# Two of four weighted sums on VectorE, and a ring that grows by a row in each tile

## The reference, cut to what matters

```
q    = (hc @ w_q).reshape(128, 8, 2, 128)                 # per tile of 128 tokens
sc   = einsum("chpd,pkd->chpk", q, subkeys)               # key scores, 2 x 128 per head
...                                                       # top 16 of each half, top 16 of their 256 sums
eidx = take_along_axis(cand_idx, top_pos)                 # 8 heads x 16 = 128 experts per token
gate = softmax(top_s)
act  = gelu(einsum("chkd,cd->chk", u_tab[eidx], hc))
out  = einsum("chk,chkd->cd", gate * act, v_tab[eidx])
```

## Time and profile before

| | |
|---|---|
| time of the kernel, median of 2 runs | 6663.14 us (6650.19 to 6676.09) |
| the profiled execution's own time | 6652.61 us |
| its span, first to last instruction | 6650.8 us |
| PE busy | 4862.6 us (73%) |
| VectorE busy | 3565.7 us (54%) |
| ScalarE busy | 849.4 us (13%) |
| GpSimd busy | 1459.3 us (22%) |
| mean rate of transfers over the span | 227 GB/s |
| gathers (queue q0) | 1342.26 MB |
| mean granted TensorE clock | 0.85 of full speed |

### The profile page before, as it was taken

One profiled execution on the slowest core, in us unless ns is written; L12 is line 12 of the kernel. 1 busy time (PEld: TensorE's weight loads), 2 busy tenths in 40 slices (PEclk: granted clock), 3 DMA queues, 4 the chain that ended last, 5 costly groups with the idle time before them and its releaser, 6 DMA issues.

```text
span 6650.8 us, 45921 instructions
## 1 busy us (share of the span) xinstructions
PE 4862.6 (73%) x14848; PEld 2726.0 (41%) x14848; DVE 3565.7 (54%) x7774; ACT 849.4 (13%) x2368; POOL 1459.3 (22%) x1310
## 2 busy tenths in 40 slices
PE   5989999966666666665579899989566666666564
PEld 3856677722222222222248567777222222222221
DVE  0755111477767677764408451114776776777544
ACT  1133000111111001110011330011111011011100
POOL 0000000033333333334300000000333333333343
PEclk8989999977777777777789899999777777777777
DMA  5100111079899988988741001110898889988886
GB/s 219 45 26 1 56 59 64 31 306 347 348 350 353 352 345 348 353 344 325 292 182 36 26 1 62 62 60 26 347 353 345 345 345 349 351 342 349 346 328 260
DMA packets 213697, 1509.71 MB, mean 227 GB/s; under 512 B 24657, under 2 KB 26961, under 8 KB 37073
## 3 DMA queue, kind: packets, MB, share of 16 engines
q0 software_dynamic: 184320, 1342.26, 52.0%
q1 hardware_dynamic: 29136, 164.52, 6.8%
HBM read 1503.54 MB, written 3.15 MB: 227 GB/s over the span
## 4 chain that ended last, share of the span: by engine, by line
PE 36%; DMA 30%; issue 12%; DVE 10%; POOL 9%; ACT 2%; DVEq 0%; SPq 0%; POOLq 0%; ACTq 0%
DMA B<-tables,R 22%; POOL B L367 9%; PE ps L600 8%; DMA R<-tables,R 6%; DVE hT L1239 4%; PE ps L440 4%; PE ps L605 4%; PE ps L657 4%; DVE B L1209 4%; PE ps L425 2%; PE ps L619 2%; DMA B<-ws 2%; PE ps L537 2%; PE ps L524 1%; PE ps L677 1%
## 5 line engine op out<-in xcount | busy, mean ns | idle before, releaser
L677 PE MATMUL ps<-B,hT 128*128 128x512 f32 x3328 | 2086.2, 790 | 1219.2 <-ACT hT L872 1219.2
L367 POOL DMA_INDIRECT B<-tables,R x1152 | 1293.7, 1123 | 4010.0 <-DVE hT L1239 2076.7
L1209 DVE SCALAR_TENSOR_TENSOR B<-B,M 128x1024 f32<-128x1024 f32 x1152 | 1389.0, 1224 | 1002.4 <-DMA B<-tables,R 971.8
L677 PEld LDWEIGHTS ps<-B,hT 128*128 128x128 f32 x3328 | 838.8, 261 | 2494.3 <-ACT hT L872 1393.1
L677 PE MATMUL ps<-R,hT 128*128 128x512 f32 x512 | 350.2, 822 | 296.7 <-ACT hT L872 296.7
L600 PE MATMUL ps<-hT,B 128*128 128x320 f32 x2048 | 561.9, 432 | 1.4 <-ACT R L831 1.4
L866 ACT ACTIVATE T<-T 128x4 f32<-128x4 f32 x320 | 66.3, 207 | 3066.7 <-DVEq L1211 3066.7
L600 PEld LDWEIGHTS ps<-hT,B 128*128 128x128 f32 x2048 | 389.0, 190 | 164.9 <-ACT R L831 3.0
L1239 DVE SCALAR_TENSOR_TENSOR hT<-B,skT,hT 128x1024 f32<-128x1024 f32 x310 | 398.1, 1284 | 40.4 <-issue 0.5
L872 ACT ACTIVATE hT<-cs,skT 128x128 f32<-128x128 f32 x960 | 317.3, 394 | 412.4 <-DVEq L1229 412.4
L1103 DVE TENSOR_TENSOR A<-ps,A 128x640 f32<-128x640 f32 x48 | 39.6, 825 | 551.2 <-PE ps L605 551.2
(11 more groups left out here) (197 smaller groups left out, 3996.3 us busy)
## 6 DMA issues: line engine op xcount, KB each, us to landing
B<-ws SPq DMA_DIRECT2D x96, 1024.0 KB, 4.9
B<-ws SPq DMA_DIRECT2D x64, 768.0 KB, 4.1
B<-tables,R POOLq DMA_INDIRECT x1152
R<-tabs SPq DMA_DIRECT2D x2, 2176.0 KB, 8.2
x<-xin SPq DMA_DIRECT2D x1, 2560.0 KB, 9.2
y<-M SPq DMA_DIRECT2D x1, 2560.0 KB, 7.9
R<-tables,R POOLq DMA_INDIRECT x128
M<-masks SPq DMA_DIRECT2D x2, 512.0 KB, 3.4
```

Of the source, the lines that this page charges most:

```text
L367: pool.indirect_dma_start(out=ring[n % RING], out_offset=None, in_=tables[:, :], in_offset=bass.IndirectOffsetOnAxis(ap=EI[:, n:n + 1], ax ...
L677: mm = pe.matmul(ps[:, bk + c, :], diag[p % DIAGS], v_row[:, c * 512:(c + 1) * 512], start=(gt == 0 and i == 1), stop=(gt == GROUPS - 1 an ...
L1209: v.scalar_tensor_tensor(out=u_row, in0=u_row, scalar=1.0, in1=h2[:, n // SLOTS, :], op0=ALU.mult, op1=ALU.mult, accum_out=dots[:, n % (2 ...
```

## The change

It moves one slot of each group from TensorE to VectorE: slots 0 and 1 are summed on TensorE, slots 2 and 3 on VectorE. The second sum of a group waits for the semaphore that the first one sets, since both add to the same accumulator. TensorE has 8 passes in a group and ScalarE two diagonal matrices.

The second edit is to the ring. A list worked out ahead gives each slot its buffer (`HOME`) and the slot that held it before (`BEFORE`). It starts with the same 10 buffers; at slot 24 of each tile the 2048 floats that held that tile's key scores are put at the front of the list of free buffers. The ring thus has 10 rows up to slot 23 of a layer, 11 from slot 24, 12 from slot 152, 13 from slot 280, 14 from slot 408 and 15 from slot 536. Buffers are taken in turn, so in this last part slot n follows slot n-15. The first gather into a new buffer waits until the eight heads of that tile are chosen. A gather into a used buffer waits for `pe_used` if the slot before was slot 0 or 1 of its group, for `dve_used` if it was slot 2 or 3.

```diff
@@ -59,8 +59,29 @@
 NG = 4
 GROUPS = SLOTS // NG
 N_GROUPS = TILES * GROUPS
-PE_G = NG - 1
-DIAGS = 2 * PE_G
+PE_G = 2
+DVE_G = NG - PE_G
+DIAGS = 6
+
+
+def rows_in_ring():
+
+    homes, before, free, last = [], [], list(range(RING)), {}
+    for n in range(N_GROUPS * NG):
+        if n % SLOTS == 6 * NG:
+            free.insert(0, RING + n // SLOTS)
+        s = free.pop(0)
+        homes.append(s)
+        before.append(last.get(s))
+        last[s] = n
+        free.append(s)
+    return homes, before
+
+
+HOME, BEFORE = rows_in_ring()
+HOMES = RING + TILES
+TURN = [HOME[:n].count(HOME[n]) for n in range(N_GROUPS * NG)]
+TURNS = [HOME.count(s) for s in range(HOMES)]
...
-        ring = [B[:, i * ROW:(i + 1) * ROW] for i in range(RING - 1)] + [R[:, 0:ROW]]
+        ring = [B[:, i * ROW:(i + 1) * ROW] for i in range(RING - 1)] + [R[:, 0:ROW]] \
+            + [A[:, t * ROW:(t + 1) * ROW] for t in range(TILES)]
...
+        got = [sig(f"got{b}", 16 * TURNS[b]) for b in range(HOMES)]
...
+        dve_used = sig("dve_used", N_GROUPS * DVE_G)
...
@@ -355,19 +377,22 @@
                 for n in range(N_GROUPS * NG):
                     if n % TOPK == 0:
                         pool.wait_ge(ei_ok.sem, ei_ok.at(l, n // TOPK + 1))
-                    if n >= RING:
-                        g, i = divmod(n - RING, NG)
-                        if i == 0:
-                            pool.wait_ge(dve_used.sem, dve_used.at(l, g + 1))
+                    if BEFORE[n] is not None:
+                        g, i = divmod(BEFORE[n], NG)
+                        if i < PE_G:
+                            pool.wait_ge(pe_used.sem, pe_used.at(l, g * PE_G + i + 1))
                         else:
-                            pool.wait_ge(pe_used.sem, pe_used.at(l, g * PE_G + i))
-                    if n == RING - 1:
+                            pool.wait_ge(dve_used.sem, dve_used.at(l, g * DVE_G + i - PE_G + 1))
+                    if HOME[n] == RING - 1 and BEFORE[n] is None:
 
                         pool.wait_ge(early_ok.sem, early_ok.at(l, 1))
+                    if HOME[n] >= RING and BEFORE[n] is None:
+
+                        pool.wait_ge(ei_ok.sem, ei_ok.at(l, (HOME[n] - RING + 1) * PH))
                     pool.indirect_dma_start(
-                        out=ring[n % RING], out_offset=None, in_=tables[:, :],
+                        out=ring[HOME[n]], out_offset=None, in_=tables[:, :],
                         in_offset=bass.IndirectOffsetOnAxis(ap=EI[:, n:n + 1], axis=0),
-                    ).then_inc(got[n % RING].sem, 16)
...
-                    for i in range(1, NG):
-                        p = g * PE_G + i - 1
-                        v_row = ring[(g * NG + i) % RING][:, D:ROW]
+                    for i in range(PE_G):
+                        p = g * PE_G + i
+                        v_row = ring[HOME[g * NG + i]][:, D:ROW]
                         pe.wait_ge(diag_ok.sem, diag_ok.at(l, p + 1))
                         for c in range(2):
                             mm = pe.matmul(ps[:, bk + c, :], diag[p % DIAGS], v_row[:, c * 512:(c + 1) * 512],
-                                           start=(gt == 0 and i == 1), stop=(gt == GROUPS - 1 and i == NG - 1))
+                                           start=(gt == 0 and i == 0), stop=(gt == GROUPS - 1 and i == PE_G - 1))
...
+                    for i in range(PE_G):
+                        p = g * PE_G + i
...
-                        u_row = ring[n % RING][:, 0:D]
-                        v.wait_ge(got[n % RING].sem, got[n % RING].at(l, (n // RING + 1) * 16))
+                        u_row = ring[HOME[n]][:, 0:D]
+                        v.wait_ge(got[HOME[n]].sem, got[HOME[n]].at(l, (TURN[n] + 1) * 16))
...
@@ -1231,13 +1256,15 @@
                 def group_sums(g):
 
                     c = g * NG % (2 * SLOTS)
-                    a, v_row = acc[g // GROUPS % 2], ring[g * NG % RING][:, D:ROW]
-                    if g % GROUPS == 0:
-                        last = v.tensor_scalar(out=a, in0=v_row, scalar1=wgt[:, c:c + 1], scalar2=None, op0=ALU.mult)
-                    else:
-                        v.wait_ge(dve_used.sem, dve_used.at(l, g))
-                        last = v.scalar_tensor_tensor(out=a, in0=v_row, scalar=wgt[:, c:c + 1], in1=a, op0=ALU.mult, op1=ALU.add)
-                    last.then_inc(dve_used.sem, 1)
+                    a = acc[g // GROUPS % 2]
+                    for i in range(DVE_G):
+                        v_row, w = ring[HOME[g * NG + PE_G + i]][:, D:ROW], wgt[:, c + PE_G + i:c + PE_G + i + 1]
+                        if g % GROUPS == 0 and i == 0:
+                            last = v.tensor_scalar(out=a, in0=v_row, scalar1=w, scalar2=None, op0=ALU.mult)
+                        else:
+                            v.wait_ge(dve_used.sem, dve_used.at(l, g * DVE_G + i))
+                            last = v.scalar_tensor_tensor(out=a, in0=v_row, scalar=w, in1=a, op0=ALU.mult, op1=ALU.add)
+                        last.then_inc(dve_used.sem, 1)
```

More of the change, by code:

```diff
@@ L252, in program @@
         ei_ok = sig("ei_ok", TILES * PH)
-        got = [sig(f"got{b}", 16 * N_GROUPS * NG // RING) for b in range(RING)]
+        got = [sig(f"got{b}", 16 * TURNS[b]) for b in range(HOMES)]
         g_exp = sig("g_exp", TILES)
@@ L357, in _ @@
                         pool.wait_ge(ei_ok.sem, ei_ok.at(l, n // TOPK + 1))
-                    if n >= RING:
-                        g, i = divmod(n - RING, NG)
-                        if i == 0:
-                            pool.wait_ge(dve_used.sem, dve_used.at(l, g + 1))
-                        else:
-                            pool.wait_ge(pe_used.sem, pe_used.at(l, g * PE_G + i))
-                    if n == RING - 1:
+                    if BEFORE[n] is not None:
+                        g, i = divmod(BEFORE[n], NG)
+                        if i < PE_G:
+                            pool.wait_ge(pe_used.sem, pe_used.at(l, g * PE_G + i + 1))
+                        else:
+                            pool.wait_ge(dve_used.sem, dve_used.at(l, g * DVE_G + i - PE_G + 1))
+                    if HOME[n] == RING - 1 and BEFORE[n] is None:
                         pool.wait_ge(early_ok.sem, early_ok.at(l, 1))
+                    if HOME[n] >= RING and BEFORE[n] is None:
+                        pool.wait_ge(ei_ok.sem, ei_ok.at(l, (HOME[n] - RING + 1) * PH))
                     pool.indirect_dma_start(
-                        out=ring[n % RING], out_offset=None, in_=tables[:, :],
+                        out=ring[HOME[n]], out_offset=None, in_=tables[:, :],
                         in_offset=bass.IndirectOffsetOnAxis(ap=EI[:, n:n + 1], axis=0),
-                    ).then_inc(got[n % RING].sem, 16)
+                    ).then_inc(got[HOME[n]].sem, 16)
         @block.tensor
```

1 line of the change is left out of this document (removed).

## The result

The changed kernel took 6050.5 us (median of 6047.71 and 6053.29) against 6663.14 us: ratio 0.905, 95% interval 0.897 to 0.914. The profiled execution took 6053.3 us with a span of 6051.5. The forecast was 6148 with a range from 6055 to 6320. The side and the mechanism were right; the gain was 600 us where 505 had been worked out, and the time lies 5 us under the range.

A forecast was written before the change was run, and what follows sets the result against it. It took gathers in flight as the bound, with VectorE and GpSimd each waiting for the other. Savings of 254 us per layer, 508 in two, less 3, taken from 6652.6 gave 6148 us; range 6055 to 6320.

The forecast's parts named there:

- The weak place: Ring, end of a group's products: only two rows can be on their way, leaving dips of 2 us per group.
- Even with 10 buffers ...: Ring: first gather waiting for VectorE's sums is 4g+12, with four rows ahead, 10.0 us of transfer, where two were 5.0.
- Adds one row in flight: Growing ring: one more row in flight from slot 24 and a fifth in the last tile.
- The second sum: VectorE, each group: the added sum costs 1.35 us, bounds 1.20 and 1.56.
- The wait left: Gather stage: 0.14 us per group of wait remains, since VectorE and transfer are close; 10.70 in tiles 0 to 3.
- VectorE's 9.21 us of work: Tiles 0 to 3: period 12.07 less 2.86 of waiting for rows leaves 9.21 us of work per group.
- The last tile: Last tile of a layer: transfer bounds at 10.01+0.14 = 10.15 us per group, from 12.79.
- My bounds: Whole kernel: sum at 1.20 with no wait gives 6062; sum at 1.56 with 0.5 of wait gives 6313.
- TensorE: TensorE's sums: 8 passes at 0.790 us, 6.3 us per group, within the period; nothing gained by fewer passes.
- The waits that stay in part: Rival, ring in tiles 0 to 3: half the wait, 1.43 us, remains; period 11.99, total 6473; chance 8%.
- neither 377 nor 353: Rivals on gather transfer: 377 GB/s over long stretches, giving 6314, chance 6%; 353 GB/s as memory's limit, giving 6602, 4%.
- A gather did not lose two instructions of VectorE: Rival, GpSimd's gathers: each loses two VectorE instructions instead of one, taking 3.73 us; total 7520; chance 2%.

The follow-up runs named there:

- experiment 1: The changed kernel's split alone, with the ring kept at 10 buffers throughout; 6118.9 us, ratio 0.913 to the kernel before.
- experiment 2: The kernel before with the growing ring alone, VectorE still summing slot 0 only; 6081.0 us, ratio 0.908 to the kernel before.
- experiment 3: The kernel before, 10 buffers, with VectorE's one slot moved from slot 0 to slot 3; 6060.4 us, ratio 0.903 to the kernel before.
- experiment 7: The changed kernel's split on a ring of 8 buffers that doesn't grow; 6963.9 us, ratio 1.039 to the kernel before.
- experiment 8: The changed kernel's split on a ring of 9 buffers that doesn't grow; 6450.2 us, ratio 0.963 to the kernel before.
- experiment 11: The kernel before with slot 3 instead of slot 0 on VectorE and 8 buffers that don't grow; 6397.4 us, ratio 0.957 to the kernel before.
- experiment 10: The changed kernel, growing ring kept, with slots 0 and 1 on VectorE instead of 2 and 3; 6187.2 us, ratio 0.926 to the kernel before.
- The last slot's kernel: Same kernel as experiment 3, timed again in five rounds beside the changed kernel; median 6039.6 us, ratio 0.903 to the kernel before.

## Why the prediction was right in its mechanism, and which terms were too slow

What failed are sizes of terms, not the loop: the wait left over in tiles 0 to 3 (0.14 forecast, none measured), VectorE's own work (9.21 forecast, 9.09 measured) and the last tile's pace (10.15 forecast, 9.71 measured). They are the same in all three traces of the changed kernel, whose stages (first to last Gelu of a layer) take 1633 to 1635 us, where before's 1937 less the 254 of the sum gives 1683. That the first measurement fell out of the range and the later ones, 6125.3 and 6112.3 us, into it is the chance of the work outside the stage; the terms were wrong in each.

**The weak place: right.** The first waiting gather had two rows in front of it, and the dips were rows running out. Experiments 1 to 3 each mend it in another way; 7, 8, 11 and the first tile of 10 bring it back in part or whole. "Even with 10 buffers ..." was the step that carried the forecast, and experiment 1 is that step alone.

**"Adds one row in flight" from the ring: right in kind, nearly nothing in size**, but with an effect in the last tile that I had not thought of.

**The second sum: 1.32 us, not 1.35.** VectorE does wait for its own signal, 0.04 after the sum's end at 4901.04.

**The wait left, 0.14 us per group: it is nought.** This is the first term that was mis-sized. I charged two stations close in speed for their unevenness. Four rows ahead leave 0.1 of it (the split alone, 10.52 against 10.41), five and more leave none. 2 x 127 x 0.14 = 36 us.

**VectorE's 9.21 us of work: too high by 0.12.** 10.41-1.32 = 9.09. I had worked it out as period less waits. The last slot's kernel, which also has waits, gives 10.15-0.93 = 9.22 by the same rule, and those without waits give 9.09. The timeline shows what the rule leaves out. In the changed kernel a product behind another starts 0.07 or 0.08 us before that one's end (4469.37+1.22 = 4470.59, the next at 4470.52). The gather between them is taken up in the last section:

```profile
4469.37 1.22 DVE L1234 SCALAR_TENSOR_TENSOR B<-B,M 128x1024 f32<-128x1024 f32 x1
...
4469.56 1.84 POOL L392 DMA_INDIRECT B<-tables,R  x1 [0.45 <-PE ps L702]
...
4470.52 1.22 DVE L1234 SCALAR_TENSOR_TENSOR B<-B,M 128x1024 f32<-128x1024 f32 x1
```

In the kernel before, one that waits for its row can't overlap, and its idle time counts only from the end of what stood in front of it (4908.75+0.08 = 4908.83, and 1.73 to 4910.56):

```profile
4908.75 0.08 DVE L1209 DVE_READ_ACCUMULATOR B<-B,M 128x1 f32 x1
...
4910.56 1.23 DVE L1209 SCALAR_TENSOR_TENSOR B<-B,M 128x1024 f32<-128x1024 f32 x1 [1.73 <-DMA B<-tables,R]
```

In tiles 0 to 3 of layer 2, 196 products behind another waited so, 1.54 per group, and 1.54 x 0.08 = 0.12 us: the whole difference. In the last slot's trace (119 waits, 1.0 per group) the same gives 0.08 of its 0.13. With the 0.03 of the sum: 2 x 127 x 0.15 = 38 us.

**The last tile, 9.71 us and not 10.15.** This is the other mis-sized term, 2 x 32 x 0.44 = 28 us. 0.14 of it is the same leftover that I charged at transfer's pace; the rest is the stock of rows. VectorE's idle time on rows, forecast at over 2 us per group there, is 1.8 for the same reason. "Transfer bounds" holds for the pace, not for the mean over 32 groups when tiles before it were bound by something slower.

Together 36+38+28 = 102 us against the 95 by which the profiled executions differ from the sum (6148-6053). My bounds had the wait at nought and the sum at 1.20, and ended at 6062. Their 10.41 us for tiles 0 to 3 is the period measured, but by luck: the work is 0.12 too high in it and the sum 0.12 too low. What they did not have at all was the stock. The edge of the range was cut to them too closely.

**TensorE.** Its passes came to 0.888 us where 0.790 had been taken, 7.1 us per group for eight, at a mean granted clock of 0.74 over the 1300 us above. That is still under the period (tiles 0 to 3 of layer 2):

```profile
L702 PE MATMUL ps<-B,hT 128*128 128x512 f32 x720 | 526.3, 888 | 447.2 <-ACT hT L897 447.2
```

**The rivals.** The waits that stay in part did not stay. The transfers hold 406 to 414 GB/s over 1200 us and more, so neither 377 nor 353 was a limit. The Trainium skill ("SBUF — State Buffer", section "Summary: rules for kernel authors") has a core count on about 358 GB/s, which the trace exceeds. The Trainium skill ("HBM Reference", section "Specifications (TRN2)") also says that a core streaming alone measures about 425, and the trace agrees with this: 4.194 MB in the 9.94 us at which most groups of the changed kernel's last tile settle in layer 1 are 422 GB/s. A gather did not lose two instructions of VectorE: gathers took 1.37 us on average in tiles 0 to 3 of layer 2, where they took 1.07, and the longest 1.99.

**What the split was for.** The forecast weighed a gain of 2 us against a price of 1.35 and took both as parts of one bargain. They are not: the place of the slot gives the gain, the number of slots on VectorE makes the price, of which the stock gives a part back in the last tile.

## What to carry to other kernels

In a ring whose buffers are freed by two engines, count how many transfers are in front of the first one that waits for the later engine; that number says more than the ring's length about whether transfers run dry, as long as the other engine's releases come early (on 8 buffers they didn't). It can be raised by giving the later engine the last slot of a group, at no cost seen here. Four rows of 1 MB ahead were nearly enough here, two were not. And where the bound changes from one stretch to the next, a buffer filled in the slower stretch makes the next one faster than its own bound for a while: take means over both.

## What was not expected of the hardware

A gather on GpSimd's queue takes 0.94 us in the changed kernel when it begins outside VectorE's products and sums (143 of the 509 in tiles 0 to 3 of layer 2). Of the 366 that begin inside such an instruction, 344 end some 0.8 us after its end, though the next one may have begun by then (the other 22 begin right at its start and take 0.94): the gather at 4469.56 in the rows above ends at 4471.40, 0.81 after the end of its product at 4470.59, inside a product that runs from 4470.52 to 4471.74. So it is held by one instruction, not by a chain of them, even at a VectorE busy for 1213 of 1300 us; the longest of the 509 took 1.99 us.

And the same dense work of TensorE ran for 120 us at half the clock in some executions and not in others, worth some 40 us, with nothing in the kernels to tell them apart there.
